# Hybrid SSD and sparse-attention decoder step: value products without the block pairs that the masks empty

## The chip, the cores and the metric

The kernel runs on one core of one Trainium2 chip. The metric is the device time of one execution in microseconds; of several executions the median is taken. No other core works beside it.

## What is computed

One layer of a decoder stack is run for a prompt group (1 sequence of 1024 tokens, width 1024) and a sample group (8 sequences of 8 tokens). Each layer has a Mamba-2 group and an attention group, which share an input and an output projection. The change touches the prompt's attention only: 8 query heads of width 64 with 2 key and value heads for each of three branches. One branch looks at block means, one ("s", selected) at the selected blocks, and one ("w", window) at a sliding window. With 16 blocks of 64 keys and the 16 best taken, the selected branch of the prompt is plain causal attention over all earlier keys. Cut to what matters:

```
qg = q.reshape(B, Tq, KV_HEADS, GQA_GROUP, HEAD_DIM)
...
ms = (top_v > -jnp.inf)[..., None] & (tok <= q_pos[None, :, None, None, None])
ps = masked_softmax(ss, ms)
o_s = jnp.einsum('bqkgns,bqknsd->bqkgd', ps, g[..., 1, :])
...
dist = q_pos[:, None] - kw_pos[None, :]
mw = (dist >= 0) & (dist <= WINDOW) & (kw_pos[None, :] >= 0)     # WINDOW = 512
pw = masked_softmax(sw, mw)
o_w = jnp.einsum('bqkgl,blkd->bqkgd', pw, kv_w[:, :, 1])
```

## The kernel before

The program is written engine by engine with semaphores set by hand. Up to about 540 us of the span come the modulation, the input projections, the Mamba-2 scan and the sample group's attention. What follows, down to the end, is the prompt's attention and the output projection. Its order is a string, `ORDER`, of one letter for each step. Every engine walks through the same list `STEPS` and carries out those letters that concern it, so TensorE (PE) works strictly in this order. The letters that matter here are `s` (step S: the scores of a unit, L2617), `x` (SOFTMAX, on DVE and ACT), `t` (TURNP: DVE turns the probabilities in blocks of 32x32, L2000), `v` (step PV: value products of one key tile, L2641), `c` (COPY: ACT evicts the sum, L1438), `k` (BACK: PE transposes it, L2651) and `o` (OUT: output projection, L2568 and L2584).

A query tile i has 128 queries (i = 0 to 7). PV is done for u = 2i (branch s, key tiles 0 to i) and u = 2i + 1 (branch w, key tiles max(0, i - 4) to i); `VALUE_TILES[u]` is the number of key tiles, and `again` counts them. In all there are 66 visits of a key tile. The probabilities lie turned in blocks of 32: partitions 32j to 32j + 31 hold, for query block j of the tile, the keys of a block b along the partitions and the 32 queries of the block for 4 heads along 128 columns. The values lie four times in SBUF (`VREP`), once for each group of 32 partitions. So one product of a pair (query block j, key block b, value head kv) uses 32 rows and 64 columns of the array: rows 32j to 32j + 31, columns 64 kv to 64 kv + 63. It writes bank 4 + j of PSUM. Eight such parts of the array (4 query blocks, 2 value heads) work beside each other.

A key tile is 4 x 4 x 2 = 32 such products, with b in the outer loop:

```
for b in range(4):
    for j in range(4):
        q, c = slice(32 * j, 32 * j + 32), again * P + 32 * b
        for kv in range(KVH):
            ins = nc.tensor.matmul(bank(4 + j, 0, P)[HALF[kv]]..., VREP[k, a + again][q, ...], PROB[k][q, ...],
                                   start=(again == 0 and b == 0), stop=(last and b == 3))
```

Each float32 product is issued to the hardware as two pairs of a weight load and a matmul, so that a key tile is 64 pairs in the trace. A transpose is one pair. PE's whole program is 8505 pairs and 349 instructions of its sequencer (waits, branches).

On the key tile that holds the queries' own positions (the diagonal tile, the last of every u) the causal mask leaves nothing where b > j. On the window's farthest tile (u odd, i >= 4, `again` = 0), where the distance may be at most 512, nothing is left where b < j. The probabilities there are exact zeros before the change too, and were multiplied like the others.

Of the kernel before, what the change touches and what calls it, by code (L numbers as in the profile page):

```python
# [49 lines left out]
WIN = 512  # L50
# [6 lines left out]
P = 128  # L57
# [79 lines left out]
def build_layer(nc, A, O, where, ncols, gate_dram, out_dram, y_dram, v_dram):  # L137
    ctx = ExitStack()
    with ctx:
# [447 lines left out]
        imp, least, cand, last, drop = (st[:, 110:126], st[:, 126:127], st[:, 128:142], st[:, 142:143], st[:, 144:160])  # L587
# [154 lines left out]
        VALUE_TILES = [min(u // 2, WIN // P if u % 2 else TT) + 1 for u in range(2 * TT)]  # L742
# [21 lines left out]
        def out_part(u, again):  # L764

            return again // 4, again % 4


        LATE = {("YTURN", 7, 0): 0, ("TURN", 7, 0): 1, ("OUT", 7, 0): 0, ("OUT", 7, 1): 1,
                ("BACK", 14, 0): 2, ("YTURN", 8, 0): 3, ("OUT", 8, 0): 2, ("OUT", 8, 1): 3}  # L770
# [7 lines left out]
        for n, ((what, u), again) in enumerate(zip(STEPS, AGAIN)):  # L778
# [26 lines left out]
            for *use, emptied_at, signal in uses:  # L805
# [5 lines left out]
                if use in LATE:  # L811
                    b = LATE[use]
# [1209 lines left out]
        def _(pe):  # L2022
# [143 lines left out]
            for i in range(TT):  # L2166
                j = i % 4
# [376 lines left out]
            for (what, u), again in zip(STEPS, AGAIN):  # L2544
                if what in ("GATE", "YSCALE", "SCALE", "RES", "SQUARE", "ROOT", "FINAL", "SUM", "COPY", "SOFTMAX", "TURNP", "CT", "WGATE", "SAMPLE"):
                    continue
                tile = MIX[u] if what in OUTPUT else None
                r = rows(tile) if what in OUTPUT else None
                if what in ("YTURN", "TURN"):
                    pe.wait_ge(s_scaled, SCALED["SCALE" if what == "TURN" else "YSCALE", u])  # L2550
                    for part in ((what,) if u in APART else ("YTURN", "TURN")):
                        bank_free(part, u, 0)
                        M = Yt(tile) if part == "YTURN" else Q3[:, tile, :]
                        for c in range(4):
                            ins = nc.tensor.transpose(use_bank(part, u, 0)[:, c * r:(c + 1) * r], M[0:r, c * P:(c + 1) * P], ident[0:r, 0:r])
                        ins.then_inc(s_fill, 1)
                    continue
                if what == "OUT" and u == 0:
                    if again == 0:
                        pe.wait_ge(s_wo_in, 16)  # L2560
                        pe.wait_ge(wload[0], 16 * WLOADS[0] + 16)
                        pe.wait_ge(*EMPTY["YTURN", u, 0])
                        bank_free("OUT", 0, 0)
                    if again == 4:
                        pe.wait_ge(*EMPTY["TURN", u, 0])
                    k = again
                    for half in range(2):
                        ins = nc.tensor.matmul(use_bank("OUT", 0, 0)[SR * half:SR * half + SR], mixT(tile, k // 4)[:, k % 4 * r:(k % 4 + 1) * r],  # L2568
                                               wo[:, k, half * 512:(half + 1) * 512], start=(k == 0), stop=(k == KT8 - 1))
                    if k == KT8 - 1:  # L2570
                        ins.then_inc(s_out, 2)
                    continue
                if what == "OUT":
                    half, n = out_part(u, again)
                    if again == 0:
                        pe.wait_ge(*EMPTY["YTURN", u, 0])
                    if half == 0 and n == 2:
                        pe.wait_ge(*EMPTY["TURN", u, 0])
                    if u == 1 and half == 0:
                        pe.wait_ge(s_wo_scaled, 2 * n + 2)  # L2580
                    if n == 0:
                        bank_free("OUT", u, half)
                    for k in range(2 * n, 2 * n + 2):
                        ins = nc.tensor.matmul(use_bank("OUT", u, half)[0:r], mixT(tile, k // 4)[:, k % 4 * r:(k % 4 + 1) * r], wo[:, k, half * 512:(half + 1) * 512],  # L2584
                                               start=(k == 0), stop=(k == KT8 - 1))
                    if n == 3:
                        ins.then_inc(s_out, 1)
                    continue
                if what == "QT":
                    if u:  # L2590
                        bank_free("QT", u, 0)
                        queries_turned(u)
                elif what == "S":
                    i, k, h, nh = UNITS[u]
                    a, n, step = keys(u)
                    if k == "c":
                        pe.wait_ge(*EMPTY["QT", i, 0])
                    if nh == 1:
                        pe.wait_ge(s_swapped, 6)
                    if u >= 2:  # L2600
                        pe.wait_ge(s_exp, u - 1)
                    base = u % 2 * 1024
                    if k == "c":
                        for g in range(GQ):
                            for kv, q in enumerate(HALF):
                                at = base + kv * 512 + g * NCB
                                ins = nc.tensor.matmul(PS[:, at:at + NCB], QD[i % 2][q, kv * GQ + g, :], KcT[q, 0:NCB], start=True, stop=True)
                        ins.then_inc(s_scores, 1)
                        continue
                    if nh > 2:  # L2610
                        for x in range(2):
                            o = PS[:, base + x * 512:base + x * 512 + nh // 2 * step].rearrange("p (h s) -> p h s", s=step)
                            nc.tensor.matmul(o, identb, masks[:, 3 * P - step:].unsqueeze(1).broadcast_to([P, nh // 2, step]), start=True, stop=False)
                    for x, pair in enumerate(zip(*score_parts(u))):
                        for half, (hh, lo, m, c) in enumerate(pair):
                            stop = nh <= 2 or x == nh // 2 - 1
                            ins = nc.tensor.matmul(PS[:, base + c:base + c + m], QD[i % 2][HALF[half], hh, :], keys_on(half, k, i, hh // GQ, lo, m),  # L2617
                                                   start=nh <= 2, stop=stop)
                    ins.then_inc(s_scores, 1)
                elif what == "CV":  # L2620
                    pe.wait_ge(s_pturned, TURNED["CT", u])
                    bank_free("CV", u, 0)
                    for h in range(AH):
                        for j in range(4):
                            q, a = slice(32 * j, 32 * j + 32), h // GQ * 256 + j * HD
                            ins = nc.tensor.matmul(use_bank("CV", u, 0)[q, h * HD:(h + 1) * HD], C[q, 32 * h:32 * h + 32], Vbd[q, a:a + HD],
                                                   start=True, stop=True)
                    ins.then_inc(s_cv, 1)
                elif what == "PV":
                    i, k = u // 2, "sw"[u % 2]  # L2630
                    a = max(0, i - WIN // P) if k == "w" else 0
                    if again == 0:
                        pe.wait_ge(s_pturned, TURNED["TURNP", LAST_TURN[i, k]])
                        pe.wait_ge(*VALUES_IN[k, i])
                        bank_free("PV", u, 0)
                    last = again == VALUE_TILES[u] - 1
                    for b in range(4):
                        for j in range(4):
                            q, c = slice(32 * j, 32 * j + 32), again * P + 32 * b
                            for kv in range(KVH):  # L2640
                                ins = nc.tensor.matmul(bank(4 + j, 0, P)[HALF[kv]].rearrange("p (g q) -> p g q", g=GQ),  # L2641
                                                       VREP[k, a + again][q, b * P + kv * HD:b * P + kv * HD + HD],
                                                       PROB[k][q, kv * GQ:kv * GQ + GQ, c:c + 32],
                                                       start=(again == 0 and b == 0), stop=(last and b == 3))
                    if last:
                        ins.then_inc(s_values, 1)
                elif what == "BACK":
                    pe.wait_ge(s_copied, u + 1)
                    bank_free("BACK", u, 0)
                    for g in range(GQ):  # L2650
                        ins = nc.tensor.transpose(use_bank("BACK", u, 0)[:, g * P:(g + 1) * P], OT[:, g * P:(g + 1) * P], ident)  # L2651
                    ins.then_inc(s_fill, 1)
# [136 lines left out]
```

## Time and profile before

| | |
|---|---|
| median of 3 runs | 885.97 us (880.46 to 892.27) |
| span of the profiled execution (first to last instruction) | 878.0 us |
| PE busy | 822.5 us (94%), 8505 matmuls |
| DVE, ACT, POOL busy | 520.0, 359.6, 259.9 us |
| value products L2641 | 4224 matmuls, from 546.9 to 847 us |

The profile gives no time of its own for the profiled execution beside its span. Its span is 2.5 us under the fastest of the three runs and 8.0 us under their median. PE is the matmul side of TensorE and PEld its weight loads, which run beside. "PEclk" is the TensorE clock granted, as a share of 2.4 GHz. Matmul ends are modelled: the record of a small matmul is some 0.27 us long although the next may start 7 to 14 ns after it.

### The profile page before, as it was taken

Reading aid. Unit: us, or ns where it says so; the run is one execution under the profiler, and the core shown is the slowest. Engines: PE = TensorE matmul, PEld = TensorE weight load, DVE = VectorE, ACT = ScalarE, POOL = GpSimd, SP = SyncE. Lnnn points to the kernel's source line nnn. Section 1 sums busy time; section 2 is a strip of 40 time slices with the busy share of each in tenths; the row PEclk is TensorE's granted clock in tenths of the full one; section 3 lists DMA queues with packets and bytes.
Section 4 is the critical chain, followed back from the end, with each engine's and each line's share of the span. In section 5 each row is a group of like instructions: output and inputs, shape, how many; then the busy total and the mean of one; then the engine's idle time right before and its main releaser. Section 6 shows DMA issues by size and latency. Waiting matters only on the chain. (4 is left out here: it accounts for less than half of the span.)

```text
span 878.0 us, 20078 instructions
## 1 busy us (share of the span) xinstructions
PE 822.5 (94%) x8505; PEld 539.5 (61%) x8505; DVE 520.0 (59%) x1095; ACT 359.6 (41%) x739; POOL 259.9 (30%) x216
## 2 busy tenths in 40 slices
PE   3999999999999999998999998888999989889996
PEld 2457998877788756657555556544646464654553
DVE  2146652376788744457435456686877867757711
ACT  4041002011222245547223337775765656444632
POOL 2048879360000043326311010446211130302021
PEclk8899999999999999999999999899999999999999
DMA  9952265454020000301942452801011010202021
GB/s 302 343 195 104 66 212 206 197 190 165 28 74 1 25 5 1 97 1 49 367 166 62 146 173 63 256 19 29 24 49 51 13 63 6 72 2 74 15 99 49
DMA packets 45411, 89.06 MB, mean 101 GB/s; under 512 B 4388, under 2 KB 26076, under 8 KB 43210
## 3 DMA queue, kind: packets, MB, share of 16 engines
q1 hardware_dynamic: 38202, 54.94, 19.3%
q0 software_dynamic: 6080, 31.79, 10.3%
q8 instruction: 68, 1.11, 0.5%
q10 hardware_dynamic: 1040, 1.05, 0.4%
q14 instruction: 21, 0.17, 0.1%
HBM read 75.49 MB, written 16.40 MB: 105 GB/s over the span
## 5 line engine op out<-in xcount | busy, mean ns | idle before, releaser
L2198 PE MATMUL PS<-W,hT 128*128 128x512 f32 x256 | 113.0, 594 | 0.5 <-DVE W L1819 0.5
L1984 DVE CUSTOM_DVE_ANT_0 PS<-PS,consts 128x640 f32<-128x640 f32 (+5 forms) x96 | 77.3, 837 | 28.7 <-PE PS L2617 28.4
L1103 POOL TENSOR_TENSOR Q<-Q,U 128x512 f32<-128x512 f32 x16 | 20.3, 1268 | 228.4 <-DVE U L2018 228.4
L2198 PEld LDWEIGHTS PS<-W,hT 128*128 128x128 f32 x256 | 47.9, 190 | 56.1 <-issue 54.8
L1431 ACT ACTIVATE hT<-PS,small 128x128 f32<-128x128 f32 (+7 forms) x64 | 47.1, 744 | 47.0 <-DVE small L1984 44.0
L2584 PE MATMUL PS<-U,Y 128*128 128x512 f32 x128 | 60.2, 604 | 0.8 <-ACT Y L1445 0.8
L2584 PE MATMUL PS<-U,Q 128*128 128x512 f32 x128 | 59.3, 601 | 1.3 <-issue 1.3
L1431 ACT ACTIVATE T<-PS,small 128x640 f32<-128x640 f32 (+4 forms) x64 | 41.9, 667 | 30.1 <-DVE small L1984 29.2
L2000 DVE STREAM_TRANSPOSE hT<-hT 128x1024 f32<-128x1024 f32 (+6 forms) x29 | 42.5, 1483 | 2.7 <-ACT hT L1431 2.6
L2584 PEld LDWEIGHTS PS<-U,Q 128*128 128x128 f32 x128 | 23.4, 190 | 32.1 <-issue 32.1
L2617 PE MATMUL PS<-KTsw,W 64*128 64x512 f32 (+3 forms) x128 | 39.4, 519 | 1.6 <-ACT hT L1431 1.3
L2584 PEld LDWEIGHTS PS<-U,Y 128*128 128x128 f32 x128 | 22.8, 190 | 27.4 <-issue 25.7
L1628 DVE SCALAR_TENSOR_TENSOR U<-T,small,U 128x512 f32<-128x512 f32 x48 | 36.1, 752 | 1.7
L2000 DVE STREAM_TRANSPOSE T<-T 128x1280 f32<-128x1280 f32 (+3 forms) x29 | 36.4, 1269 | 1.1 <-ACT T L1431 1.0
L2617 PE MATMUL PS<-KTsw,T 64*128 64x320 f32 (+3 forms) x128 | 33.1, 446 | 0.9 <-ACT T L1431 0.7
L2093 PE MATMUL PS<-T,hT 128*128 128x512 f32 x64 | 31.3, 635 | 1.1 <-DVE hT L1466 1.1
L2153 PE MATMUL PS<-W,U 128*128 128x144 f32 (+1 forms) x192 | 32.1, 317 | 0.0
L1559 DVE TENSOR_TENSOR Q<-PS,Q 128x256 f32<-128x256 f32 x28 | 11.5, 423 | 32.3 <-PE PS L2153 31.9
L2247 PE MATMUL PS<-hT,W 128*128 128x256 f32 x128 | 30.5, 382 | 0.0
L1933 DVE TENSOR_TENSOR W<-PS,W 128x512 f32<-128x512 f32 x16 | 10.9, 683 | 32.4 <-PE PS L2584 32.3
L2153 PEld LDWEIGHTS PS<-W,U 128*128 128x128 f32 x192 | 28.4, 190 | 1.7
L1131 POOL TENSOR_TENSOR W<-W 128x1024 f32<-128x1024 f32 (+1 forms) x8 | 18.8, 2353 | 35.5 <-ACT W L1416 29.3
(545 smaller groups left out, 1855.3 us busy)
## 6 DMA issues: line engine op xcount, KB each, us to landing
W<-in_w_in SPq DMA_DIRECT2D x4, 2048.0 KB, 7.7
W<-in_w_ada SPq DMA_DIRECT2D x7, 1024.0 KB, 16.1
U<-in_x_prompt SPq DMA_DIRECT2D x8, 512.0 KB, 11.3
W<-in_w_ada SPq DMA_DIRECT2D x2, 2048.0 KB
U<-in_state_win_kv POOLq DMA_DIRECT2D x8, 512.0 KB
W<-in_x_prompt SPq DMA_DIRECT2D x8, 512.0 KB, 3.5
out_y_prompt<-W SPq DMA_DIRECT2D x8, 512.0 KB, 3.4
out_new_win_sample<-in_state_win_kv POOLq DMA_DIRECT2D x1, 4032.0 KB, 24.1
```

What stands on the lines that cost most here:

```text
L1103: nc.gpsimd.tensor_tensor(Q3[:, i, :], Q3[:, i, :], spare, ALU.add).then_inc(s_added, 1)
L1131: nc.gpsimd.tensor_tensor(x, x, fin_g[0:rows(MIX[u])].rearrange("p (h c) -> p h c", h=2), ALU.mult).then_inc(s_added, 1)
L1431: ins = act.activation(PROB[k][:, hh, 0:n * P], S[:, m, :], ACT.Exp, bias=sneg_m[u % 2][:, m:m + 1], scale=-1.0, accum_out=dsum[i % 2][:, ...
L1628: ins = nc.vector.scalar_tensor_tensor(o, r[:, k:k + 512], w, o, ALU.mult, ALU.add)
L1984: ins = nc.vector.tensor_tensor_reduce(x, x, strip(u), 1.0, -NEG, ALU.add, ALU.min, sneg_m[u % 2][:, m:m + 1])
L2000: ins = nc.vector.transpose(x, x)
L2093: ins = nc.tensor.matmul(bank(i), hT3[:, k, i * P:(i + 1) * P], Wkv[:, k, :], start=(k == 0), stop=(k == KT8 - 1))
L2153: ins = nc.tensor.matmul(slot(n, m), left, right, start=(k == 0), stop=(k == 3))
L2198: ins = nc.tensor.matmul(bank(z_bank(u)), hT3[:, k, i * P:(i + 1) * P], w, start=(k == 0), stop=(k == KT8 - 1))
L2247: ins = nc.tensor.matmul(out, left[:, h], right, start=(k == 0 and m in (1, 2, 7)), stop=(k == 3), skip_group_check=m in (3, 4, 5, 6))
L2584: ins = nc.tensor.matmul(use_bank("OUT", u, half)[0:r], mixT(tile, k // 4)[:, k % 4 * r:(k % 4 + 1) * r], wo[:, k, half * 512:(half + 1) * ...
L2617: ins = nc.tensor.matmul(PS[:, base + c:base + c + m], QD[i % 2][HALF[half], hh, :], keys_on(half, k, i, hh // GQ, lo, m), start=nh <= 2, ...
```

## The change

Which pairs of blocks are multiplied is now told by a function. For a diagonal tile query block j takes key blocks 0 to j, for the far tile of the window j to 3, and for all others 0 to 3. A product left out is not issued. The start flag goes to the first product that is issued for a bank, and the stop flag to the last. The list of steps, the waits and the signals stay.

```diff
+        def key_blocks(u, again, j):
+
+            if again == VALUE_TILES[u] - 1:
+                return 0, j + 1
+            if u % 2 and u // 2 >= WIN // P and again == 0:
+                return j, 4
+            return 0, 4
+
...
                     for b in range(4):
                         for j in range(4):
+                            lo, hi = key_blocks(u, again, j)
+                            if not lo <= b < hi:
+                                continue
                             q, c = slice(32 * j, 32 * j + 32), again * P + 32 * b
                             for kv in range(KVH):
...
-                                                       start=(again == 0 and b == 0), stop=(last and b == 3))
+                                                       start=(again == 0 and b == lo), stop=(last and b == hi - 1))
```

On PE at the window branch of query tile 5 (key tiles 1 to 5; `Vw` and `Y` hold the values of one tile for each 32 products) stands before:

```order
L2617 MATMUL PS<-KTsw,T 128x448
L2641 MATMUL PS<-T,Vw 64x128 x32
L2641 MATMUL PS<-T,Y 64x128 x64
L2617 MATMUL PS<-KTsw,T 128x320
L2617 MATMUL PS<-W,T 128x320 x2
L2617 MATMUL PS<-KTsw,T 128x320
L2641 MATMUL PS<-T,Y 64x128 x32
L2641 MATMUL PS<-T,Vw 64x128 x32
```

and in the same place after the change:

```order
L2625 MATMUL PS<-KTsw,T 128x448
L2652 MATMUL PS<-T,Vw 64x128 x20
L2652 MATMUL PS<-T,Y 64x128 x64
L2625 MATMUL PS<-KTsw,T 128x320
L2625 MATMUL PS<-W,T 128x320 x2
L2625 MATMUL PS<-KTsw,T 128x320
L2652 MATMUL PS<-T,Y 64x128 x32
L2652 MATMUL PS<-T,Vw 64x128 x20
```

The far tile at the head and the diagonal tile at the end go from 32 products to 20; nothing changes its place. At the end of PE's program, where the last diagonal tile of branch s and all of branch w of query tile 7 are (OUT in between), stands before:

```order
L2641 MATMUL PS<-T,Y 64x128 x64
L2584 MATMUL PS<-U,Q 128x512 x2
L2641 MATMUL PS<-T,Vw 64x128 x64
L2641 MATMUL PS<-T,Y 64x128 x32
L2584 MATMUL PS<-U,Q 128x512 x2
```

and after:

```order
L2652 MATMUL PS<-T,Y 64x128 x52
L2592 MATMUL PS<-U,Q 128x512 x2
L2652 MATMUL PS<-T,Vw 64x128 x64
L2652 MATMUL PS<-T,Y 64x128 x20
L2592 MATMUL PS<-U,Q 128x512 x2
```

Here again only the counts of the far tile (one of the first two) and of the diagonal tile differ.

## Rows read from the trace of the kernel before

**Rows 1.** The page: busy time, and the granted clock in 40 slices.

```profile
PE 822.5 (94%) x8505; PEld 539.5 (61%) x8505; DVE 520.0 (59%) x1095; ACT 359.6 (41%) x739; POOL 259.9 (30%) x216
...
PEclk8899999999999999999999999899999999999999
```

**Rows 2.** The longest waits from 540 us: who waited for whom, us, times, longest.

```profile
DVE W L1933 <- PE PS L2584: 32.3, 9, 9.9
...
ACT OTb L1438 <- PE PS L2641: 30.1, 12, 6.8
...
DVE PS L1984 <- PE PS L2617: 28.4, 18, 3.6
```

**Rows 3.** The value products' line: what ended PE's idle time before them (us, times).

```profile
  issue: 11.1, 12
  DVE hT L2000: 2.9, 2
```

**Rows 4.** Line L2641 alone by stretch: length, PE busy, PEld busy, granted clock, DMA.

```profile
555.20:556.50 1.30, 1.21 (x64) 0.96 (x64) 1.00 1.20 197
566.80:570.30 3.50, 3.42 (x128) 3.18 (x128) 0.56 1.06 326
584.20:586.30 2.10, 2.08 (x128) 1.84 (x128) 1.00 0.04 8
```

**Rows 5.** Timeline: seven output matmuls of 512 columns, back to back.

```profile
597.37 3.17 PE L2584 MATMUL PS<-U,Y 128*128 128x512 f32 x7
```

**Rows 6.** Timeline of PE, and once PEld: what began after a wait for "issue".

```profile
572.52 0.49 PE L2651 MATMUL PS<-consts,OTb 128*128 128x128 f32 x3 [1.05 <-issue]
593.72 0.48 PE L2641 MATMUL PS<-hT,Vs 32*64 32x128 f32 x17 [1.49 <-issue]
629.85 1.76 PEld L2641 LDWEIGHTS PS<-hT,Y 32*64 32x64 f32 x118 [0.24 <-issue]
669.82 0.43 PE L2641 MATMUL PS<-hT,Vs 32*64 32x128 f32 x3 [1.36 <-issue]
673.74 0.48 PE L2641 MATMUL PS<-hT,Y 32*64 32x128 f32 x16 [0.30 <-issue]
703.49 0.80 PE L2641 MATMUL PS<-T,Y 32*64 32x128 f32 x36 [1.33 <-issue]
716.22 0.59 PE L2641 MATMUL PS<-hT,Y 32*64 32x128 f32 x22 [0.48 <-issue]
749.25 0.59 PE L2641 MATMUL PS<-T,Y 32*64 32x128 f32 x25 [0.52 <-issue]
786.63 0.59 PE L2641 MATMUL PS<-T,Y 32*64 32x128 f32 x25 [0.88 <-issue]
842.01 1.55 PE L2584 MATMUL PS<-U,Q 128*128 128x512 f32 x3 [1.27 <-issue]
```

**Rows 7.** Timeline of PE from 759.5 us: the two waits in branch s of query tile 6.

```profile
759.50 0.27 PE L2641 MATMUL PS<-hT,Y 32*64 32x128 f32 x1
759.52 0.28 PE L2641 MATMUL PS<-hT,Vs 32*64 32x128 f32 x2
759.54 0.27 PE L2641 MATMUL PS<-hT,Y 32*64 32x128 f32 x1
...
762.15 0.91 PE L2641 MATMUL PS<-hT,Y 32*64 32x128 f32 x39 [1.97 <-issue]
...
769.60 0.99 PE L2641 MATMUL PS<-hT,cmpm 32*64 32x128 f32 x48 [1.38 <-issue]
```

**Rows 8.** The page: the DMA queue of instructions (packets, MB, share of 16 engines).

```profile
q8 instruction: 68, 1.11, 0.5%
```

**Rows 9.** All engines from 545 us, PE alone: length, busy, granted clock, DMA.

```profile
545.00:550.00 5.00, 3.45 (x82) 0.60 1.01 302
565.00:570.00 5.00, 3.12 (x120) 0.66 1.05 290
575.00:580.00 5.00, 5.00 (x26) 1.00 0.00 0
```

## The prediction

> **What bounds the kernel now.** I read the page first: PE is busy for 94% of the span, DVE 59%, ACT 41%, and the granted clock is full from the second half on [rows 1]. Then the waits from 540 us, where the change works: the long ones are DVE and ACT waiting for PE, 28 to 32 us for each of three lines [rows 2]. So PE's own stream sets the time there, and a microsecond that PE loses or saves moves the end with it, as long as nobody else comes late. Last I asked for the changed line alone. Before the value products PE waited little for DVE (2.9 us in all), but 11.1 us in 12 waits for "issue", that is for nothing which the profile shows [rows 3]. These waits are the heart of the matter.
>
> **What a key tile costs the array.** Two tiles back to back, 128 pairs of weight load and matmul, take 2.08 us [rows 4]; less 0.27 us for the modelled end that is 1.81 us, 0.91 us a tile or 14.2 ns a pair. Is that the price of issuing 64 pairs, or of the array? Eight parts of the array work beside each other, so each gets 8 of the 64 matmuls. A matmul of 512 columns takes (3.17 - 0.60) / 6 = 0.43 us in a dense row [rows 5], so 128 columns take 0.107 us, and 8 of them 0.86 us. That is the tile, nearly. And where the mean clock was 0.56, the same 128 pairs took 3.42 us instead of 2.08 us [rows 4]: it follows the clock. So a tile costs what the fullest part of the array has to do.
>
> The change takes 12 of 32 products from a tile, but not from every part. On the diagonal tile query block 3 keeps all four key blocks, on the far tile query block 0 does. Its part still has 8 matmuls in a row: 0.86 us. **Direct saving on the array: nothing**, for 20 tiles (16 diagonal, 4 far). At the other end stands a tile whose time falls with its pairs: 24 pairs x 14.2 ns = 0.34 us, 6.8 us over 20 tiles. Between these ends I take nothing, since the clock row and the 512-column row both speak for the array. Below nothing I see no reason: no product is added and no wait.
>
> **What the issue waits are.** Their places are not random. From the start at 762.15 us to the one at 769.60 us lie 255 pairs by the timeline (39, 4, 64, 4 and so on), that is 510 instructions and two of the sequencer, twice 256 [rows 7]. The queue of instructions brought 68 packets with 1.11 MB [rows 8], and PE's program is 2 x 8505 + 349 = 17,359 instructions, 255 a packet. So PE's program comes in blocks of 256, and PE stands still at the head of a block that is not there yet. How fast can a block follow another? 769.60 - 762.15 = 7.45 us for two is 3.7 us [rows 7]; 673.74 - 669.82 = 3.9 us [rows 6]. A block of value products alone takes the array 128 x 14.2 ns = 1.8 us. Value products use up the program twice as fast as it comes: 3.7 us / 256 = 14.5 ns an instruction against the 7.1 ns they need. Output matmuls (0.43 us a pair) let the supply catch up.
>
> The idle times of rows 6 and 7 add up to 12.0 us (two short ones, 0.24 and 0.20 us, are not shown). Each hides 0.25 us more, because idle time is counted from the modelled end of a matmul: 11 x 0.25 = 2.8 us. So about 15 us of PE's time are lost for want of instructions. This is what the change can win from.
>
> The Trainium skill speaks to this ("Runtime: NRT & Kernel Launch", section "Instruction fetch mechanics"): each engine's instruction memory is refilled in blocks of 16 KiB, 256 instructions, while the block before is executed, and crossing a boundary is called mostly hidden, since dispatch is slower than the refill. The block size agrees with rows 8; "mostly hidden" does not agree with rows 6 and 7. By that sentence alone the sum would be nothing.
>
> **The sum.** A trimmed tile has 24 pairs = 48 instructions less. Where the supply is what PE waits for, each is worth 14.5 ns: 0.70 us a tile. Where no wait follows before the next calm passage, it is worth nothing. So I went through the dense passages and counted the trimmed tiles ahead of a wait [rows 6, 7]:
> - 547 to 573 us: three, one of them (567 us) close ahead of the wait at 572.5: 1 tile.
> - 584 to 595 us: two, one ahead of 593.7: 1 tile.
> - 620 to 632 us: two; the window's is ahead of a short wait at 629.8 us, 0.24 us on the weight loads [rows 6]: that much at most.
> - 656 to 676 us: two; the window's is ahead of 669.8, the other ends the passage: 1 tile.
> - 700 to 723 us: three; far and diagonal tile of the window ahead of 703.5 to 716.2: 2 tiles.
> - 746 to 771 us: three; far and diagonal tile of the window ahead of 749.2, 762.2, 769.6: 2 tiles.
> - 783 to 791 us: two; the far tile is ahead of 786.6: 1 tile.
> - 822 to 847 us: three; two ahead of 842.0: 2 tiles.
>
> 10 tiles x 0.70 + 0.24 = 7.2 us. As a cross-check I laid PE's whole list out in blocks of 256, with the traced start-to-start times less the issue waits, and let each block be ready 3.6 us after the first instruction of the one before: waits of 14.3 us before, 7.4 us after, so 6.9 us saved. Asking for the next block 32 instructions into one, ready 3.05 us later, gave 14.9 and 5.4 us, so 9.5 us. Of the saving I take off some 0.7 us, because PE then comes earlier to the waits for DVE that are now short [rows 3]. **Forecast: 6.5 us less.** Against the profiled execution that is a span of 878.0 - 6.5 = 871.5 us; against the median 885.97 - 6.5 = 879.5 us. The span of the traced execution lies 8 us under the median, of which 2.5 us are below even the fastest run; I carry the difference over unchanged.
>
> The waits and order of steps stay as they are, so DVE, ACT, POOL and the data transfers get nothing to do or to wait for that is new; they only move earlier with PE.
>
> **Rivals.**
> *A tile's array time falls too.* For it: in rows 7 matmuls of the next tile (Y) start before the last ones of this one (Vs), so the parts do not march in step; where a far tile is followed by full ones, query blocks that are ahead could stay ahead. Query block 0 has the most in the far tile and the least in the diagonal one, so over a whole window u the loads are even (34 matmuls each instead of 40). Against it: instructions are handed out in order, and a part that is behind soon holds up the others. If all of it came: 6.8 + 7.2 = 14 us, 872 us.
>
> *Nothing is gained.* The waits at block heads move to other places, or DVE and ACT take over as the ones that are late. For it: DVE is busy most of the time in these passages, and moving all block boundaries in my layout by 80 to 96 instructions made the waits grow by up to 3.5 us rather than fall. Against it: nothing ahead of 547 us changes, so the boundary at the first trimmed tile stays where it is. Gain 0 to 2 us: 885 us. The Trainium skill's "Runtime: NRT & Kernel Launch", with its mostly hidden crossings, would have it so as well.
>
> *Slower: the clock.* Around the first value products the granted clock is 0.60 and 0.66 in stretches of 5 us [rows 9], that is part of the time at 1.2 instead of 2.4 GHz; by 575 us it is full. The first trimmed tiles (547, 555, 567 us) lie just there, and they would give the array 37% less to do in them. If the low clock came back or stayed on, each microsecond of PE's work would cost one more: 575 to 580 us is 5.0 us of solid work [rows 9]. It decides once more than 6.5 us of work fall under it; with 15 us it costs 15 - 6.5 = 8.5 us, 894 us. Against it: the array's fullest part is as long at work as before, and the clock recovered after the 567 us tiles although PE had waited for DVE just before them [rows 3].
>
> **How the numbers follow.** Forecast (supply of instructions alone) 0.62; array time falls too, in part or whole, 0.15; nothing gained 0.17; slower by the clock 0.06. The runs before spread from 880 to 892 us, so a median of few runs adds some 3 to 4 us either way. The range goes from 868 us (the first rival less 4) to 889 us (nothing gained plus 4). 2% is 17.7 us, which is about what a measurement of this kernel can tell from no change: faster than 868.3 us needs all of the first rival and a low draw, 0.06; slower than 903.7 us needs over 24 us under the low clock, 0.02; within 2% 0.92.
>
> **What would show it.** PE has 8025 matmuls instead of 8505, and the instruction queue 64 packets instead of 68. In passages without waits a trimmed tile still takes 0.9 us from its first start to the next line's: if it takes 0.55 us, the first rival holds. The waits for issue at line L2652 fall from 11.1 us to about 5 us, and still stand 256 instructions apart. The blocks still follow each other at no less than 3.3 to 3.9 us. If the waits for issue stay near 11 us, or as much new waiting for DVE and ACT appears, the forecast is wrong.

## The result, and the profile after

Over 11 runs of each, the changed kernel takes 875.3 us (872.25 to 878.45) where the kernel before takes 884.9 us (878.4 to 892.3). The ratio is 0.9882, with a 95% interval of 0.9859 to 0.9905: 1.2% or some 10 us faster, which is clear of noise but within the 2% named in the forecast. The forecast was 6.5 us less, with a range of 868 to 889 us, and "within 2%".

The page of the changed kernel, with the lines that answer to [rows 1] and [rows 8]:

```profile
span 873.5 us, 19118 instructions
...
PE 822.3 (94%) x8025; PEld 538.9 (62%) x8025; DVE 519.2 (59%) x1095; ACT 358.9 (41%) x739; POOL 260.2 (30%) x216
...
q8 instruction: 64, 1.05, 0.5%
```

PE's busy time over the whole span hardly moved (822.5 to 822.3 us), although 480 matmuls are gone; by stretch, below, it looks a little different. The instruction queue brings four packets less. What ended PE's idle time before the line of the value products (now L2652), and before one other line, which answers to [rows 3] (us, times, longest):

```profile
PE PS L2652 <- issue: 6.7, 9, 1.4
PE PS L2652 <- DVE hT L2008: 2.9, 2, 2.1
...
PE PS L2634 <- issue: 0.5, 1, 0.5
```

The waits for "issue" on PE after 540 us went from 13.7 us (11.1 at the value products, 1.3 and 1.3 at two other lines) to 7.2 us. The wait for DVE stayed at 2.9 us.

The first value product starts at 551.6 us here and at 546.9 us before. The part ahead of it is the same program, and was 4.7 us slower in this execution; from there to the end it takes 873.5 - 551.6 = 321.9 us instead of 878.0 - 546.9 = 331.1 us, that is 9.2 us less. This agrees with the ratio. The two spans alone (4.5 us apart) would have misled: on record each execution's span is some 1.8 us under its time, so the traced execution of the kernel before took about 880 us, among its fastest, and that of the changed kernel 875.3 us, its median. PE alone from the first value product to the end, before and after (length, busy, granted clock, DMA):

```profile
546.90:878.00 331.10, 300.60 (x5576) 0.98 0.18 56
551.60:873.50 321.90, 297.91 (x5096) 0.99 0.18 58
```

So 6.5 us of the 9.2 us are idle time that went, and 2.7 us busy time. The busy part is not work of the array either, as far as it can be traced. Each wait hides 0.25 us in the modelled end of the matmul before it, and there are 10 waits now instead of 15: 1.25 us. The rest is of the size of one difference in the clock: it was at half for 6.8 us at the first value products before (546 to 553 us) and for 3.4 us in this execution, worth 1.7 us at most. A second trace of the changed kernel (e10 below) had the low clock of the kernel before there, and took 322.2 us.

Two rows of the line by stretch, which answer to [rows 4], and four waits, which answer to [rows 7]:

```profile
587.60:589.80 2.20, 2.08 (x104) 1.86 (x104) 1.00 0.00 0
709.80:712.00 2.20, 2.08 (x128) 1.87 (x128) 1.00 0.21 65
```

```profile
748.11 0.47 PE L2652 MATMUL PS<-T,Y 32*64 32x128 f32 x15 [1.09 <-issue]
...
758.77 0.55 PE L2652 MATMUL PS<-hT,Vs 32*64 32x128 f32 x20 [1.42 <-issue]
...
762.69 0.68 PE L2652 MATMUL PS<-hT,Y 32*64 32x128 f32 x28 [0.80 <-issue]
...
766.52 0.70 PE L2652 MATMUL PS<-hT,hst 32*64 32x128 f32 x32 [0.82 <-issue]
```

The first pair is the clearest reading of the case. A full tile and a trimmed one are 104 matmuls and take 2.08 us; two full tiles are 128 matmuls and take 2.08 us as well. Both at full clock and with nothing to wait for: leaving out 12 of 32 products saves nothing. In the timeline three starts after a wait stand 3.92 and 3.83 us apart (758.77, 762.69, 766.52), one block of instructions each: between the first two lie 20 + 5 + 3 + 59 + 4 + 36 = 127 matmuls with their weight loads.

### The profile page after: what moved, and what is told of

It is laid out like the page before. It is cut to its first block and busy times, and to the rows that moved or that the text cites. A ratio compares the mean times of both kernels' runs of the same rounds, so it can differ in the third digit from the quotient of the medians.

```text
span 873.5 us, 19118 instructions
## 1 busy us (share of the span) xinstructions
PE 822.3 (94%) x8025; PEld 538.9 (62%) x8025; DVE 519.2 (59%) x1095; ACT 358.9 (41%) x739; POOL 260.2 (30%) x216
## 3 DMA queue, kind: packets, MB, share of 16 engines
q0 software_dynamic: 6080, 31.79, 10.4%
q8 instruction: 64, 1.05, 0.5%
q10 hardware_dynamic: 1040, 1.05, 0.4%
```

## The experiments

The theory to be tested (S): PE waits at the head of each block of 256 instructions that has not come yet, and the gain is what of these waits goes. The rival (A): the gain comes from products that the array no longer does. Ratios are to runs of the kernel before on the same chip. "Waits" is the sum of PE's idle time that ended with "issue", after 540 us, in the profiled execution, and "value part" that execution's time from its first value product to the end. The ratios are from 6 to 12 runs of each kernel, waits and value part from one.

| run | ratio (95%) | waits, us | value part, us |
|---|---|---|---|
| before | 1 | 13.7 | 331.1 |
| changed | 0.9882 (0.9859 to 0.9905) | 7.2 | 321.9 |
| e1 changed, 56 pads | 1.0043 (1.0008 to 1.0079) | 12.0 | 331.4 |
| e2 before, 56 pads | 1.0009 (0.9978 to 1.0039) | 14.6 | 333.0 |
| e3 thin products | 1.0011 (0.9981 to 1.0040) | 16.4 | 337.3 |
| e4 balanced | 0.9838 (0.9801 to 0.9876) | 7.1 | 319.7 |
| e5 changed, 128 pads | 0.9884 (0.9840 to 0.9928) | 6.9 | 322.5 |
| e6 before, 92 pads | 0.9999 (0.9971 to 1.0027) | 14.6 | 333.7 |
| e7 diagonal tiles alone | 0.9886 (0.9831 to 0.9941) | 9.0 | 326.4 |
| e8 far tiles alone | 1.0001 (0.9970 to 1.0032) | 14.9 | 331.7 |
| e9 paired | 0.9846 (0.9813 to 0.9879) | 9.4 | 322.7 |
| e10 changed again | 0.9862 (0.9811 to 0.9913) | 6.9 | 322.2 |
| e11 paired again | 0.9870 (0.9818 to 0.9922) | 7.9 | 323.5 |

Where the waits stand can be counted in the traces themselves. Take PE's instructions in order of time, weight loads and those of its sequencer included, and number them. The 13 traces have 165 waits for "issue" after 540 us. Of these, 139 end at the same place in every 256 instructions (remainder 193 to 195), whatever the kernel and the padding. The other 26 are the same two in every trace, 0.17 and 0.99 us, at the same two matmuls wherever the blocks begin (584.20 and 626.24 us in the kernel before); what they wait for no run shows. That leaves 12.5 us at block heads in the kernel before and 6.1 us in the changed one. The traces also hold the packets of the instruction queue [rows 8]. Each of the 139 waits ends 1.0 to 1.7 us after such a packet has landed (median 1.4 us), the other 26 end 2.1 us or more after one. In the kernel before, a packet lands at 760.70 us, PE starts at 762.15, the next packet begins at 763.69 and lands at 764.74. So PE waits for the block that this queue brings.

**e1, e2, e5: move the block heads, leave the work.**

```diff
             mod(0)
+            for _ in range(56):
+                nc.tensor.transpose(bank(3, 0, 9)[0:9], ident[0:9, 0:9], ident[0:9, 0:9])
             for p in range(4):
```

e1 on the changed kernel:

> The changed kernel with 56 small transposes (9x9, 112 instructions of PE) added at about 18 us, where PE waits 3.9 us anyway. Nothing of the value products changes, only where the heads of the blocks of 256 instructions fall. Theory S (supply of instructions): the gain depends on these places. My block layout gives waits of 16 us instead of 7.2 us, so about 9 us more than the changed kernel: a ratio to the kernel before of 0.995 to 1.003. Theory A (the gain comes from products that the array no longer does): as the changed kernel, 0.988.

e2 on the kernel before:

> The kernel before with the same 56 transposes. Theory S: the layout gives waits of 12.7 to 13.6 us instead of 14.3 to 15.5 us, so 2 us less than before: ratio 0.998, between 0.994 and 1.001, and no slower than the padded changed kernel, the order of the two turned round. Theory A: 1.000, and the padded changed kernel 1.2% faster than this one.

e5, the control, with `range(128)` on the changed kernel:

> Control for the pads: the changed kernel with 128 small transposes (256 instructions, one whole block) in the same idle place at the start. The block heads fall on the same instructions of the value products as without pads. Theory S: ratio as the changed kernel, 0.988 (0.986 to 0.992). If pads cost by themselves, or through the clock, what 56 of them cost, 128 cost more: ratio over 1.004.

In e1's timeline the pads lie where PE had nothing to do:

```profile
13.95 1.55 PE L2086 MATMUL PS<-consts 9*9 9x9 f32 x56
17.54 1.12 PE L2093 MATMUL PS<-consts,U 128*128 128x128 f32 x4 [2.04 <-DVE U L1471]
```

They take 1.55 us, and PE still waits 2.04 us behind them. Yet 600 us later the whole gain is gone: 1.0043. The control says that it is not the pads themselves: with 128 of them, a whole block, the ratio is 0.9884, that of the changed kernel. So where the blocks begin decides over the gain, as theory S has it, since the three kernels do the same value products in the same order and differ in nothing else there. But e1 came out worse than was expected (1.0043, above 0.995 to 1.003), and with smaller waits (12.0 us, not 16). Four of its waits, in order:

```profile
621.27 0.87 PE L2654 MATMUL PS<-T,Y 32*64 32x128 f32 x16 [0.85 <-issue]
...
632.64 0.54 PE L2654 MATMUL PS<-hT,Y 32*64 32x128 f32 x5 [1.72 <-issue]
...
715.34 0.44 PE L2654 MATMUL PS<-hT,Vs 32*64 32x128 f32 x5 [1.65 <-issue]
...
845.07 0.76 PE L2654 MATMUL PS<-T,Y 32*64 32x128 f32 x22 [1.22 <-issue]
```

Between 620 and 634 us the kernel before had one wait at a block head, 0.24 us on the weight loads; e1 has three (the one that is not shown is 0.81 us at 628.64 us).

The waits are not all that e1 lost. Its value part is 9.2 us longer than that of e10, the trace of the changed kernel whose low clock at the first value products is the same. The waits are 5.1 us of that, and four more of them hide 1.0 us. The rest is of the size of a difference in the clock: twice it fell to half for 3.4 us, at 717 and at 847 us, where e10 had it full. Each costs 1.7 us at most, 3.4 us together. The first, PE alone:

```profile
717.00:720.50 3.50, 3.50 (x61) 0.53 0.08 30
```

Both began within 2 us after the end of a wait shown above (1.65 us at 715.34, 1.22 us at 845.07). The traces of e2, e4, e6, e7 and e8 have one such stretch each between 600 and 865 us, all of them 1 to 2 us after a wait of 1.4 to 1.8 us at a block head. The other traces have none, and waits as long passed without one (1.97 us at 762.15 us in the kernel before). So a wait may cost more than its own length; that it brings the low clock is not shown. The traced execution was also the fastest of the 12 of e1 (880.6 us; median 887.9 us), so that what the slower ones lost is not seen in it.

e2 was expected 2 us faster than before and was not (1.0009, at the edge of 0.994 to 1.001); that the padded changed kernel is no faster than the padded kernel before (1.0043 against 1.0009) came as expected.

**e3: the instructions back, without their work.**

```diff
+                            q, c = slice(32 * j, 32 * j + 32), again * P + 32 * b
                             if not lo <= b < hi:
+                                for kv in range(KVH):
+                                    nc.tensor.matmul(bank(4 + j, 384, 392)[HALF[kv]],
+                                                     VREP[k, a + again][q, b * P + kv * HD:b * P + kv * HD + HD],
+                                                     PROB[k][q, kv * GQ, c:c + 8], start=True, stop=True)
                                 continue
-                            q, c = slice(32 * j, 32 * j + 32), again * P + 32 * b
```

> The changed kernel, but each product left out is replaced by one of 8 columns into unused columns of the same bank: PE's instruction count is that of the kernel before again (8505 matmuls), the array's work almost that of the changed kernel. Theory S: all of the gain goes, ratio 1.00 (0.997 to 1.003), waits for issue in the same places as before. Theory A: 0.988 to 0.990.

1.0011: all of the gain goes when the instructions come back without their columns. Its waits fall on the same instructions as those of the kernel before, all 13 that stand at block heads, and on four heads more (16.4 us instead of 13.7). Its value part is the longest of the table also for 6.8 us at half clock from 575 us on. Of the 13 waits, the one that stood at 593.72 us ahead of the last 17 matmuls of a tile [rows 6] now stands at 598.97 us, ahead of 17 again.

```profile
598.97 0.48 PE L2656 MATMUL PS<-hT,Vs 32*64 32x128 f32 x17 [1.76 <-issue]
```

**e4: same count, shorter chain in the array.**

```diff
             if again == VALUE_TILES[u] - 1:
-                return 0, j + 1
+                return 0, 3 - j % 2
             if u % 2 and u // 2 >= WIN // P and again == 0:
-                return j, 4
+                return 0, 3 - j % 2
```

> The changed kernel with another choice of pairs: on diagonal and far tiles query blocks 0 and 2 take key blocks 0 to 2, query blocks 1 and 3 take 0 and 1. The count is 20 products as in the changed kernel, but the fullest part of the array has 3 key blocks instead of 4; so it leaves out pairs that the reference needs and takes others. If the fullest part sets a tile's time, a trimmed tile takes 0.65 us instead of 0.87 us from first to last start where nothing waits. Theory S: in dense passages that only lengthens the waits for issue; over all 20 tiles 0 to 2.5 us less than the changed kernel, ratio 0.985 to 0.988. Theory A: 20 x 0.21 = 4.3 us less, ratio 0.983.

```profile
586.06 1.82 PE L2652 MATMUL PS<-T,Vw 32*64 32x128 f32 x104 [0.17 <-issue]
```

Full and trimmed tile together now take 1.82 us; the same 104 matmuls took 2.08 us in the changed kernel. The difference of 0.26 us is a little over two matmuls of 0.107 us, the part of the chain that is gone. So the fullest part of the array does set a tile's time, where instructions are there. The ratio of 0.9838 is that of theory A in the comparison to the changed kernel, but its interval (0.9801 to 0.9876) reaches far into that of S. From the first value product to the end its trace takes 319.7 us, 2.2 us less than that of the changed kernel and 2.5 us less than e10's, whose low clock at the first value products is the same. It has one stretch of 3.4 us at half clock more than e10 (757 us), worth 1.7 us at most, so that its own saving is 2.5 to 4.2 us: the upper edge of theory S's 0 to 2.5 us, up to the 4.3 us of theory A. How the two limits share these passages is not shown.

**e6, e7, e8: how well does the block layout give sizes?** e6 is e2 with `range(92)`; e7 leaves the far tile's two lines out of `key_blocks`, e8 the diagonal tile's.

> The kernel before with 92 small transposes (184 instructions) in the same place. This is the shift at which my block layout loses most on the kernel before: waits of 21 to 22 us instead of 14.3 to 15.5 us. Theory S: 6 to 8 us slower than before, ratio 1.007 to 1.009. Theory A: 1.000.

> The change on the 16 diagonal tiles alone (192 of the 240 products left out). Theory S: the block layout gives waits of 7.9 to 10.5 us instead of 14.3 to 15.5 us, 5 to 6.5 us less, ratio 0.993 to 0.994. Theory A: 80% of the gain, 0.9905.

> The change on the window's 4 far tiles alone (48 of 240 products). Theory S: waits of 11.3 to 13.4 us instead of 14.3 to 15.5 us, 2 to 3 us less, ratio 0.9965 to 0.998: a far tile has always other tiles and a block head behind it, so each gives 0.5 to 0.7 us. Theory A: 20% of the gain, 0.9976.

Not well by the ratios. e6 was to be 6 to 8 us slower and is not (0.9999), with waits of 14.6 us instead of 13.7. e7 brings all of the gain (0.9886) where 5 to 6.5 us were expected, e8 nothing (1.0001) where 2 to 3 us were. Theory A does no better with e7 and e8: 80% and 20% of the gain is not what they show, though its 0.9905 and 0.9976 lie within the intervals. The traces are kinder to e7: its value part is 4.7 us shorter than that of the kernel before, with a stretch of 3.4 us at half clock in it, and the interval of its ratio just takes in the 0.994 that was expected. What holds in all three is that the trace with few waits goes with the low ratio: 14.6 and 14.9 us stand at 1.00, 9.0 us at 0.989. The block layout holds for the places of the waits (in e6 14 of the 16 waits are at block heads), but not their sum.

**e9, e11, e10: can the array's chain be shortened with the right products?** In the window units with a far and a diagonal tile, query block 0 has 4 key blocks in the one and 1 in the other, query block 3 the reverse. Issued side by side each has 5.

```diff
+                    if k == "w" and i >= WIN // P:
+                        far, own = ([x for x in every if x[0] == t] for t in (0, 4))
+                        by = {j: [x for x in far if x[2] == j] + [x for x in own if x[2] == j] for j in range(4)}
+                        parts = [[by[j][m] for m in range(5) for j in range(4)]]
+                        parts += [[x for x in every if x[0] == t] for t in (1, 2)]
+                        parts += [[x for x in every if x[0] == 3 and x[1] // 2 == h] for h in range(2)]
...
```

> The changed kernel with another order of the same products in the 4 window units that have both a far and a diagonal tile: the 40 products of the two are issued first and block by block, so that every query block has 5 in a row, and the other 3 tiles follow over the remaining 4 steps. All products and the instruction count of the changed kernel stay (8025 matmuls). The array's chain falls from 16 to 10 matmuls of 0.107 us for the two tiles, 0.64 us a unit, 2.6 us in all where nothing waits. If the supply of instructions sets these passages (block heads stand where they stood), little comes of it: 0 to 1 us less than the changed kernel, ratio 0.987 to 0.989. If the array's fullest part sets them, 2.6 us: 0.985.

> The paired kernel of e9 once more. In e9's trace only units w of query tiles 4 and 7 got shorter (0.77 and 0.65 us), those of 5 and 6 not, since a wait for instructions took the place of the array's. Theory S: 1.4 us less than the changed kernel beside it, ratio 0.985 to 0.988. If the array's chain counted in full it were 2.6 us: 0.985.

> The changed kernel once more, on the same chip as the paired one, so that the two can be set side by side: ratio 0.988 (0.985 to 0.991).

The last window unit, in the changed kernel and in e9:

```profile
839.58 2.06 PE L2652 MATMUL PS<-T,Vw 32*64 32x128 f32 x126
...
841.43 1.13 PE L2652 MATMUL PS<-T,Y 32*64 32x128 f32 x38
```

```profile
833.02 2.32 PE L2660 MATMUL PS<-T,Y 32*64 32x128 f32 x144
...
837.19 2.10 PE L2660 MATMUL PS<-T,Vw 32*64 32x128 f32 x128
```

The changed kernel's second step there (two full tiles and the diagonal tile) takes 2.98 us, its first 2.09 us; e9 takes 2.32 and 2.10 us for the same products. That is the 0.65 us that were worked out. In units 5 and 6 longer waits at block heads took its place (in e9 1.65 us instead of 1.09 in unit 5, 1.18 and 0.21 us instead of 0.83 in unit 6). Side by side, e10 and e11 read 0.9862 and 0.9870: no difference that these runs can tell. Whether the paired order is worth a microsecond stays open.

## Why the prediction was right, and where it was not

- **PE's stream sets the time; the waits for "issue" are what can be won.** Right. The kernels of the table fall into two groups: seven with waits of 6.9 to 9.4 us stand at 0.984 to 0.989 with value parts of 320 to 326 us, six with 12.0 to 16.4 us (the kernel before among them) at 1.000 to 1.004 with 331 to 337 us. Within a group the ratio does not follow the waits: e1 has the least waits of its group and the highest ratio.
- **A trimmed tile costs the array what it cost before.** Right to the digit: 2.08 us for 104 as for 128 matmuls. This rested on the 512-column row and on the row at 0.56 of the clock [rows 4, 5]. The rival of falling array time is out where the two can be compared; e4 shows what would have to be done for it.
- **Blocks of 256, 3.7 us each.** Right: 139 waits stand at one place of 256 instructions, and in the rows shown the blocks follow at 3.8 to 3.9 us. Of 46 pairs of waits at neighbouring heads in the 13 traces 39 stand 3.4 to 4.3 us apart, the others further. e1, e3 and e5 show what it is worth, by moving blocks without work and by bringing instructions back without work.
- **The Trainium skill's "mostly hidden" crossings** ("Runtime: NRT & Kernel Launch", "Instruction fetch mechanics"). The measurement decides: between e1 and the changed kernel, which differ by a shift of these crossings by 112 instructions, lie 1.6%. The size of a block, 256 instructions, agrees.
- **The sum of 6.5 us.** The mechanism held and the size was small: 10.4 us by the ratio, 9.6 us between the two medians, 9.2 us by the two traces. The term "10 tiles x 0.70", with 0.24 us beside it 7.2 us, came out nearly in sum: 6.4 us of idle time at block heads went, and with the hidden quarters of five waits 7.6 us. By passage it did not, so that this sum is in part luck:

| passage of before, us | expected | idle time at heads that went |
|---|---|---|
| 547 to 573 | 0.70 | 1.05 |
| 584 to 595 | 0.70 | 1.73 |
| 620 to 632 | 0.24 (weight loads) | 0 on PE |
| 656 to 676 | 0.70 | 0.81 |
| 700 to 723 | 1.40 | 1.52 |
| 746 to 771 | 1.40 | -0.26 |
| 783 to 791 | 0.70 | 0.05 |
| 822 to 847 | 1.40 | 1.47 |

I took each wait as the buyer of the tiles ahead of it within its own passage. But removed instructions also shift every later block head, by up to 960 instructions. Three waits of before (572.5, 587.9 and 593.7 us) fell away whole; between 746 and 771 us the new waits (1.09, 1.42, 0.80 and 0.82 us) are as large as the old. What the forecast lacked against the 9.2 us is the 0.7 us taken off for DVE, some 0.4 us of waits, and up to 1.7 us of clock, which fell differently in the two traces. The cross-check by layout gave 6.9 or 9.5 us; against the 7.6 us of the waits the first is the nearer, and e6, e7 and e8 show that neither gives sizes reliably. At the value products' own line the waits fell from 11.1 to 6.7 us, where about 5 us had been named.
- **0.7 us taken off for DVE.** Not seen: the wait for DVE is 2.9 us as before.
- **The clock.** The low stretches came again, some 5 us later, with the whole program, the first of them shorter in this execution, and the clock was full from 575 us on (from 570 us before [rows 9]); the rival played no part in the changed kernel. In e1 and five others the low clock came back later, as told there. PE alone by stretch (length, busy, granted clock, DMA):

```profile
555.00:560.00 5.00, 5.00 (x59) 0.78 1.04 355
...
570.00:575.00 5.00, 4.18 (x108) 0.66 1.05 311
575.00:580.00 5.00, 4.51 (x88) 1.00 0.10 36
```

The spread of the runs is mostly this clock. Of the runs of the kernel before that were taken beside the experiments, 11 had a mean granted clock of 0.992 or more and took 880.5 us in the mean (879.2 to 883.4), 12 had 0.982 or less and took 889.3 us (886.2 to 892.1). The changed kernel's 11 runs lie closer together (0.983 to 0.991). The clock is no rival for the gain: the means of the two kernels are 0.988 and 0.986, by these figures 1 to 2 us of the 10 (an estimate).

What stays open: what decides when the clock falls, and why e1 lost more at the median than in its trace.

## What to carry to other kernels

When PE works through many small matmuls, ask first how fast its program arrives: here 256 instructions in 3.7 to 3.9 us, at least 29 ns for a pair of weight load and matmul. Here a product that was left out where the array's fullest part stayed as full saved only its instructions, and those counted only where PE ran out of them. And a gain or loss of one per cent in such a kernel can come from where blocks of instructions begin: a whole-block pad and a part-block pad tell that apart from a real effect.

## What was not expected of the hardware

A pad of 56 matmuls of 9 columns, 1.55 us in an idle place 600 us earlier, took the whole gain of 10 us away, about a third of it in the trace by stretches at half clock, and 128 of them took nothing. That a blocked supply can undo a change altogether was in the forecast only as a rival with 0.17.
